# Norms with the tokens on partitions, and another start for the first unit, in a two-block forward kernel

## The reference

```
x = x + 0.5 * swiglu(rms(x, ffn1_norm), w1, w3, w2)          # ffn1, hidden width 2816
x = x + (gate_a * rwkv7(h) + gate_b * fox(h)) @ w_out        # h = rms(x, mix_norm)
x = x + 0.5 * swiglu(rms(x, ffn2_norm), ...)                 # ffn2
x = rms(x, final_norm)
mod = silu(c) @ w_ada + b_ada                                # shifts, scales and gates of block two
x   = x   + 0.5 * g1 * swiglu(rms(x, .)   * (1 + sc) + sh, ...)   # ffn3, main tokens
ctx = ctx + 0.5 * g1 * swiglu(rms(ctx, .) * (1 + sc) + sh, ...)   # ffn3, 256 context tokens, same weights
x = x + g2 * merge(retention(x, ctx), fourier(x))            # ret_q, ret_k, ret_v, four_in, ... out2
x = x + 0.5 * g3 * swiglu(rms(x, .) * (1 + sc) + sh, ...)    # ffn4
return rms(x, norm_final)
```

## Time and profile before

| | |
|---|---|
| median of 3 runs | 1769.89 µs (1769.77 to 1769.99) |
| the profiled execution | 1771.81 µs, its span 1770.0 µs |
| PE busy | 1704.9 µs, 96% of the span |
| DVE, ACT busy | 1059.6 µs (60%), 652.3 µs (37%) |
| granted TensorE clock, mean over the span | 0.991 of full |
| read from HBM | 265.48 MB, 151 GB/s over the span |

### The profile page before, as it was taken

One profiled execution on the slowest core, in us unless ns is written; L12 is line 12 of the kernel. 1 busy time (PEld: TensorE's weight loads), 2 busy tenths in 40 slices (PEclk: granted clock), 3 DMA queues, 4 the chain that ended last, 5 costly groups with the idle time before them and its releaser, 6 DMA issues.

```text
span 1770.0 us, 32228 instructions
## 1 busy us (share of the span) xinstructions
PE 1704.9 (96%) x13366; PEld 1552.1 (88%) x13366; DVE 1059.6 (60%) x1570; ACT 652.3 (37%) x763; POOL 5.2 (0%) x13
## 2 busy tenths in 40 slices
PE   6999999899999999999999999899999999999997
PEld 6999898676998999998888888888889799989997
DVE  6766747542766766765465465942356634676766
ACT  4333446222544333432222212522346334443332
POOL 0000000000000000000000000000000000000000
PEclk9999999999999999999999999999999999999999
DMA  6545566476244545422222222232223235445551
GB/s 245 190 175 185 193 257 240 152 283 256 100 165 171 190 168 187 166 85 105 95 95 95 95 95 96 95 119 104 90 96 106 97 143 185 176 151 184 185 190 48
DMA packets 37537, 267.74 MB, mean 151 GB/s; under 512 B 4192, under 2 KB 4448, under 8 KB 5456
## 3 DMA queue, kind: packets, MB, share of 16 engines
q1 hardware_dynamic: 36432, 262.37, 40.8%
q0 software_dynamic: 1024, 4.17, 0.6%
HBM read 265.48 MB, written 1.05 MB: 151 GB/s over the span
## 4 chain that ended last, share of the span: by engine, by line
PE 92%; DVE 4%; ACT 2%; issue 1%; DMA 1%; DVEq 0%; POOL 0%; SPq 0%; ACTq 0%
PE PS L329 25%; PE PS L330 24%; PE PS L331 24%; PE PS L542 2%; PE PS L543 2%; PE PS L544 2%; PE PS L562 2%; PE PS L981 2%; PE PS L407 1%; PE PS L1014 1%; PE PS L1001 1%; ACT W_HI L316 1%; PE PS L783 1%; DVE RSTD L1467 1%; PE PS L968 1%
## 5 line engine op out<-in xcount | busy, mean ns | idle before, releaser
L329 PE MATMUL PS<-H_HI,W_HI 128*128 128x256 f32 (+1 forms) x2128 | 652.0, 306 | 21.0 <-DVE H_LO L1459 11.9
L330 PE MATMUL PS<-H_LO,W_HI 128*128 128x256 f32 (+1 forms) x2128 | 647.0, 304 | 0.0
L331 PE MATMUL PS<-H_HI,W_LO 128*128 128x256 f32 (+1 forms) x2128 | 646.8, 304 | 0.0
L316 ACT ACTIVATE W_HI<-RAW 128x2048 fp32r<-128x2048 f32 x213 | 407.2, 1912 | 585.0 <-PE PS L331 553.9
L324 DVE TENSOR_TENSOR W_LO<-RAW,W_HI 128x2048 fp32r<-128x2048 f32 x213 | 487.3, 2288 | 189.4 <-ACT W_HI L316 188.9
L329 PEld LDWEIGHTS PS<-H_HI,W_HI 128*128 128x128 f32 x2128 | 411.2, 193 | 43.8 <-issue 27.6
L330 PEld LDWEIGHTS PS<-H_LO,W_HI 128*128 128x128 f32 x2128 | 411.5, 193 | 15.4 <-issue 0.2
L331 PEld LDWEIGHTS PS<-H_HI,W_LO 128*128 128x128 f32 x2128 | 411.1, 193 | 14.9
L329 PE MATMUL PS<-HID_HI,W_HI 128*128 128x256 f32 (+1 forms) x704 | 218.4, 310 | 3.3 <-DVE XC L1509 3.3
L330 PE MATMUL PS<-HID_LO,W_HI 128*128 128x256 f32 (+1 forms) x704 | 217.9, 309 | 0.0
L331 PE MATMUL PS<-HID_HI,W_LO 128*128 128x256 f32 (+1 forms) x704 | 217.8, 309 | 0.0
(11 more groups left out here) (315 smaller groups left out, 1713.8 us busy)
## 6 DMA issues: line engine op xcount, KB each, us to landing
RAW<-stream SPq DMA_DIRECT2D x249, 1024.0 KB, 4.8
XC<-xin SPq DMA_DIRECT2D x2, 512.0 KB, 5.0
XC<-xin POOLq DMA_DIRECT2D x1, 1024.0 KB, 5.1
out<-NT POOLq DMA_DIRECT2D x2, 512.0 KB, 2.9
CON<-consts POOLq DMA_DIRECT2D x1, 548.0 KB, 6.0
LW<-lora POOLq DMA_DIRECT2D x1, 512.0 KB, 6.6
DFT<-dft POOLq DMA_DIRECT2D x1, 512.0 KB, 3.8
ROPE<-rope POOLq DMA_DIRECT2D x1, 256.0 KB, 3.4
```

What stands on the lines that cost most here:

```text
L316: nc.scalar.activation(W_HI[s % RING][:], RAW[u % RING][:], ACT.Copy).then_inc(hi_done, 1)
L329: nc.tensor.matmul(acc, w_hi, x_hi, start=first, stop=False)
L330: nc.tensor.matmul(acc, w_hi, x_lo, start=False, stop=False)
L331: return nc.tensor.matmul(acc, w_lo, x_hi, start=False, stop=last)
```

## The change

The norms get their sums with the tokens on the partitions. PE takes the squares as the fixed operand and a vector of ones as the moving one (`ONE3`, two columns wide), a half of the tokens at a time, and leaves 128 by 2. Root and reciprocal run on 128 by 2. Then PE spreads the result over the partitions again with two matmuls against the identity (`norm_spread`), and DVE scales from PSUM. All eight tiles are scaled, then all eight low halves made; the first unit behind a norm starts with the products of `H_HI` and multiplies `H_LO` behind them. nd and ne become one chain: eight sums with four columns (the squares and the squares times the square of nd's gain) within `up_ctx(0)`, and the norm ne is gone as a pass of its own. In front of ffn2 and ffn4 two of the three sums go into the last output tile, and `keep_clock` issues matmuls whose result nobody reads around the third.

The rest: four transfers for the first tokens and two for unit 0, whose `W_LO` GpSimd makes and PE multiplies last; seven matmuls on a constant at the start (`WARM`); the split of the second unit behind a norm moves behind the last addition into `XC`; the last `down` of ffn3 does the main tokens and then the context (`down_last`), the norm ng between them; `ret_q` has other banks, nh other places; one `w_ada` unit moves from in front of `fox_qk` into the inversion (`ada(16)`); SP stores the output in four transfers.

```diff
-ADA_INV = 23
-ADA_AFTER = {PHASE["fox_qk"] - 1: 3, PHASE["fox_v"] + 1: ADA_INV}
+ADA_INV = 24
+ADA_AFTER = {PHASE["fox_qk"] - 1: 2, PHASE["fox_v"] + 1: ADA_INV}
...
+            for q in range(4):
+                sp.dma_start(XC[:, 0, 2 * q:2 * q + 2], xin[0, :, 2 * q:2 * q + 2]).then_inc(S(f"x_in{q}"), 16)
...
+            for h in range(2):
+                sp.dma_start(by_k(RAW[0])[:, :, 4 * h:4 * h + 4], by_k(stream[0])[:, :, 4 * h:4 * h + 4])\
+                    .then_inc(landed[0] if h else S("half_in"), 16)
...
+            for k in range(0, KT, 2):
+                sp.wait_ge(S("final"), k + 2)
+                sp.dma_start(out[:, k:k + 2], NT[:, k:k + 2]).then_inc(S("stored"), 16)
...
+            pool.wait_ge(S("half_hi"), 1)
+            pool.wait_ge(hi_done, 1)
+            nc.gpsimd.tensor_tensor(W_LO[0][:], RAW[0][:], W_HI[0][:].bitcast(F32), ALU.subtract).then_inc(lo_done, 1)
             pool.dma_start(CON[:, 256:], consts[:, 256:]).then_inc(S("masks_in"), 16)
...
                 pe.wait_ge(S("norm_sq"), KT * NORM[name] + k + 1)
-                last = nc.tensor.matmul(NORM_BANK[name], con("ones"), tmp[:, k], start=(k == 0), stop=(k == 7))
+                w = 4 if name == "nd" else 2
+                for tt in range(2):
+                    last = nc.tensor.matmul(sums(name), tmp[:, k, tt * P:(tt + 1) * P], SQW[:, k, 2 - 2 * tt:6 - 2 * tt] if w == 4 else
+                                            ONE3[:, 1 - tt:3 - tt], start=(k == first and tt == 0), stop=(k == last_k and tt == 1))
...
+            def keep_clock(n, bank):
+                for _ in range(n):
+                    nc.tensor.matmul(BK8[bank][:, 0:ROWS], con("ident"), CON[:, 0:ROWS], start=True, stop=True)
+            def norm_spread(name):
+                pe.wait_ge(S("norm_rec"), NORM[name] + 1)
+                for q in ((2, 3, 0, 1) if name == "nd" else (0, 1)):
+                    last = nc.tensor.matmul(spread_of(name)[:, q * P:(q + 1) * P], RSTD[:, q:q + 1].to_broadcast([P, P]), con("ident"),
+                                            start=True, stop=True)
+                last.then_inc(S("norm_spread"), 1)
...
+                            if t == 0 and k % 2:
+                                norm_sum("nd", 4 * w + k // 2)
...
+                    if t == 0:
+                        for k in range(KT):
+                            pe.wait_ge(S("norm_hi"), KT * NORM_H[h_name] + k + 1)
+                            for w in range(2):
+                                c = (w * KT + k) * P
+                                two(tile(w), W_HI[sl][:, c:c + P], W_LO[sl][:, c:c + P], H_HI[:, 0, k], k == 0)
+                    if t == 0:
+                        for k in range(KT):
+                            pe.wait_ge(S("norm_h"), KT * NORM_H[h_name] + k + 1)
...
+                    for q, t in ([(q, 0) for q in range(4)] + [(q, 1) for q in range(4)] +
+                                 [(q, t) for q in range(4, 16) for t in range(2)]):
+                        h, m = q // 8, q % 8
...
+                        if q == 9:
+                            norm(then)
+                        if q == 11:
+                            norm_spread(then)
...
                 if halves == 2:
                     up_ctx(0)
-                    norm(h_name)
-                    up_ctx(1)
+                    up_ctx(1, (0,))
+                    norm_spread("nd")
+                    up_ctx(1, (1,))
...
+            pe.wait_ge(S("warm_in"), 1)
+            for _ in range(7):
+                nc.tensor.matmul(BK8[0][:, 0:ROWS], WARM[:, 0:P], WARM[:, P:P + ROWS], start=True, stop=True)
+            pe.wait_ge(S("one3"), 1)
+            for k in (6, 7, 0):
+                norm_sum("na", k, first=6, last_k=0)
             pe.wait_ge(S("con_in"), 16)
-            norm("na")
+            keep_clock(1, 0)
+            norm_spread("na")
+            keep_clock(2, 0)
             ffn(0, "ffn1", 1, "na", "nb")
-            ada(12)
+            ada(4)
+            norm_spread("nb")
+            ada(4)
...
             for n in range(NC):
                 z_step(n)
-            ada(12)
+            ada(16)
...
-                 behind={3: lambda: norm("nc")})
+                 within={(7, 4): lambda: norm_sum("nc", 0), (7, 6): lambda: norm_sum("nc", 6)})
+            keep_clock(2, 0)
+            norm_sum("nc", 7)
+            keep_clock(1, 0)
+            norm_spread("nc")
+            keep_clock(2, 0)
...
-            split_hi(act, 0)
+            act.wait_ge(S("half_in"), 16)
+            A(by_k(W_HI[0])[:, :, 0:4], by_k(RAW[0])[:, :, 0:4], ACT.Copy).then_inc(S("half_hi"), 1)
+            act.wait_ge(landed[0], 16)
+            A(by_k(W_HI[0])[:, :, 4:8], by_k(RAW[0])[:, :, 4:8], ACT.Copy).then_inc(hi_done, 1)
...
             def norm_rows(name, half, gain, shift=None, tmp=NT):
-                for k in range(KT + 2):
-                    if k < KT:
-                        scale(name, half, k, gain, tmp)
-                    if k >= 2:
-                        rest(name, half, k - 2, shift, tmp)
+                dve.wait_ge(S("norm_spread"), NORM[name] + 1)
+                for k in range(KT):
+                    scale(name, half, k, gain, tmp)
+                for k in range(KT):
+                    rest(name, half, k, shift, tmp)
...
-                split_lo(dve, s0 + 34)
-                add(10, range(8), m0 + 124)
+                if halves == 1:
+                    add(10, range(8), m0 + 124)
...
-            split_lo(dve, 0)
             norm_rows("na", 0, lambda k: par("n1", k))
+            dve.wait_ge(lo_done, 1)
             split_lo(dve, 1)
...
-            norm("nb", 0, lambda k: par("nm", k))
+            split_lo(dve, PHASE["fox_qk"] + 1, part=0)
+            reciprocal("nb")
+            split_lo(dve, PHASE["fox_qk"] + 1, part=1)
+            norm_rows("nb", 0, lambda k: par("nm", k))
```

277 lines of the change are left out of this document (206 added, 71 removed).

## The result

The changed kernel took 1759.08 us (median of 4 runs, 1758.39 to 1759.72) against 1769.83 before: ratio 0.9941, 95% interval 0.9926 to 0.9957. It is faster, by 10.8 us where 18.7 were forecast, and lies 1.1 us outside the range.

A forecast was written before the change was run, and what follows sets the result against it. PE was taken as the bound, busy 1704.9 of 1770.0 µs and waiting nearly always for norms. Gains of 24.3 less costs of 5.6 gave 18.7, so 1753.1 profiled and a median of 1751.2; range 1747 to 1758.

The forecast's parts named there:

- The fourth `w_ada` unit: In the inversion: its load must wait for a free buffer, so PE waits 3.2 µs, plus 1.0 for the clock.
- nd, ne and ng: Norms: nd and ne as one chain, gain 2.8 µs; ng under the context's tiles, with what follows, gain 4.5.
- End: Last norm and output store: shorter reciprocal and root, an added spread, smaller last transfer; gain 2.2 µs.
- One of the signs that I had set for being wrong: At the start, unit 1 of ffn1 waiting for GpSimd beyond 20 µs would show the forecast wrong.
- Start: First norm and unit 0 of ffn1: GpSimd's subtraction taken as 2.29 µs, unit 1 at 19.9 instead of 26.3, gain 6.4.
- The rival that the two hold each other up: At the start, DVE's low halves wait for GpSimd's subtraction: nothing lost, 1752.1 to 1753, or 1761 µs; chance 0.17.
- The rival's price, 20.8: When unit 1 of ffn1 begins if GpSimd takes twice DVE's time and holds up its low halves: 20.8 µs.
- Costs: Losses at nf (a spread, 0.4 µs) and in the inversion (an added `w_ada` unit, its wait and clock): 5.6 in all.
- The rival "the clock is not held": Small sums count as PE idle: gain gone at nc and ni, half speed at nb, nd or ng; 1757 to 1759, chance 0.14.
- nc and ni: Norms before ffn2 and ffn4: two sums inside the last tile, high pass first, no 1.2 GHz; gains 2.7 and 1.7 µs.
- nb: Norm behind ffn1: 1.66 wait gone, last addition +0.7, first product +4.15; gain 4.0 µs, 0.93 of it only moved.
- The base: Whole kernel: profiled execution before took 1771.8 µs, and the median was taken to lie 1.9 under it.

The follow-up runs named there:

- e12: Changed kernel with the moved `w_ada` unit behind the first unit of `fox_qk` instead of in the inversion: 1757.26 µs, ratio 0.9935 to the kernel before.
- e1: Changed kernel with unit 0's low half made by DVE behind its token low halves, GpSimd computing nothing: 1759.35 µs, ratio 0.9942 to the kernel before.
- e3: Changed kernel with four dense `keep_clock` products in PE's wait in front of the sums of nf: 1756.85 µs, ratio 0.9927 to the kernel before.
- e8: Changed kernel with GpSimd making only half of unit 0's low half, DVE the rest behind its token low halves: 1759.64 µs, ratio 0.9943 to before.
- e6: Changed kernel with three dense fp32 products in PE's wait in front of the sums of nb: 1759.24 µs, ratio 0.9943 to the kernel before.
- e2: Changed kernel with the `w_ada` units where they stood before, three behind ffn1 and three in the inversion: 1759.78 µs, ratio 0.9943 to before.
- e4: Changed kernel with the first two sums of nc and ni behind the last tile, not inside it: 1755.89 µs, ratio 0.9918 to before.
- e7: Changed kernel with the sums of nc and ni behind the last tile and no `keep_clock` at either: 1759.32 µs, ratio 0.9943 to before.
- e9: Changed kernel with the edits of e3, e4, e6, e8 and e12 together: 1746.73 µs, ratio 0.9879 to the kernel before.

## Why the prediction was right or wrong

Right: the direction, and about half of the places. **The fourth `w_ada` unit** waited 3.30 us (forecast 3.2), with 1.1 lost to the clock behind it (1.0); e12 shows both to be the price of that place. **nd, ne and ng** came to 3.29 and 4.48 against 2.8 and 4.5. The reciprocal is 0.17, the 1.66 gaps are gone, the clock is 1.00 behind ng and ni (at ni it fell in e1 and e3, with the same code there), and the tile of `out` waits 0.92 inside (1.0). **End**: 2.87 against 2.2. The norm gave 1.1 of the 1.25 expected; from the end of the last scaling to the end of the span it is 2.64 us instead of 4.40, 1.8 less, where I had allowed 0.95 for the transfers.

Wrong, by step. The sum misses 6.6 us, 3.2 of them at the start, 1.6 at nc, 1.4 at nf, 1.3 at nb and 0.6 at ni, less what nd, ne, the end and the inversion gave beyond the forecast. One of the signs that I had set for being wrong, unit 1 waiting for GpSimd beyond 20, came true.

- **Start, "Its floor is DVE's for the same tile, 2.29 ... I take 2.29, the same form".** It is 4.57, and I had set the longer time aside because by it "the sum stays". The Trainium skill, GPSIMD Engine Reference, "3. Performance versus the Vector engine", gives 4497 ns, and the trace agrees with its 4.57 us. The sum stays only if GpSimd's time lies beside DVE's. The rival that the two hold each other up was the true case, and my forecast had the overlap wrong: the first low half took 2.93 instead of 0.41, and e1 shows why. The Trainium skill, SBUF — State Buffer, "Who interferes with whom", says that a VectorE instruction with two SBUF inputs contends with a GpSimd one that reads SBUF, and that one with at most one SBUF input, outside the modes that use two ports, doesn't; by that rule both come out right, the low halves held up and the scalings of e8 (one operand in PSUM) at 3.22. The low half was held to the end of GpSimd's instruction, and 0.29 beyond.
  The rival's price, 20.8, was too small by 2.3. GpSimd started 1.4 later than the 11.2 of the forecast: "Unit 0 has landed whole at about 10.0" was read from the kernel before, where the unit is one transfer, and the change has two, behind two more for the tokens; the second half landed at 11.38. With that the low halves ended at 19.82 instead of 18.5 and the split of unit 1 at 22.02 instead of 20.8. The last 1.1 is the clock, for which the forecast's own sum had charged 1.6. That the scaling started at 11.40, not 10.0, cost nothing more, as the first low half ended with GpSimd's row in any case.
- **Costs, "nf gets a spread, 0.4".** The spread costs that (e3). But I had looked for a lost clock only where PE waits over 4 us. At nf the same wait of 1.69 had left the clock at 1.00 in front of wide sums and doesn't in front of sums of 2 columns. The rival "the clock is not held" named the mechanism, and put it at nc and ni, nb, nd and ng, not at nf. What it costs at nf is 1.6 in this profile and 3.1 in six others. That rival's time, 1757 to 1759, lies close to the 1759.08 measured, by luck: of its terms only a part of nc's is in this profile, and nearly half of the sum's miss lies at the start, which it left as it was.
- **nc and ni, "PE waits there 1.0 µs inside the tile and the third sum comes 1.7 later" and "no 1.2 GHz".** The third sum came 2.6 later, since the clock wasn't held and `keep_clock` stood in front of it at 1.2 GHz; where the clock held (e6) it came 2.0 later. nc gained 1.1 for 2.7, 1.0 of the miss for the clock. At ni the clock held, the third sum came 2.0 later there too, and the gain was 1.1 for 1.7; the rest of that wasn't looked at. That the sums should never have been in the tile (worth 1.5 at each) I hadn't asked.
- **nb, "last addition +0.7".** It was +1.7: I took the additions to follow PE, where DVE alternates them with the squares at 0.67 a block, in the kernel before too. The first product came at +5.6 instead of +4.15, and the gain was 2.7 for 4.0. I had also not seen that the moved split frees its buffer of the stream 6 us later, counted from the start of `down` (load issued 10.6 us behind it instead of 4.5); the change doesn't pay for it at nb, since it has one `w_ada` unit less there, but in the inversion, where that unit went.
- **The base.** 1.3 us: the profiled execution of before stood 1.98 over its median, the other 0.64. That is the spread between executions and no fault of the mechanism.

## What to carry to other kernels

- When narrow instructions replace wide ones on TensorE behind a wait, look at the granted clock there, however short the wait: at nf it fell in ten of ten profiles behind 1.69 us of waiting and 12 matmuls of 2 columns, and in none of three with dense products in that wait. Look at every place that has the new form, not only at the long gaps.
- A unit that is moved out of one stall needs a place with dense work in front of it and a free buffer. And an instruction that frees a buffer can't be moved later for nothing: ask which load waits for it. With the split moved behind the additions, the load that had been issued at 209.48 was issued at 213.22 (e2).
- GpSimd was help for VectorE under instructions that take an operand from PSUM (e8); beside two-input ones from SBUF its work held them up (e1). And an instruction put inside a tile to save time behind it delays that tile, on which the whole tail hangs.
- A landing read from the kernel before holds only while the transfers ahead of it stay as they are.

## What the runs showed that was not expected

The clock falls at different places in executions of the same code. nb held it in the change, in e4 and in e7 and lost it in seven others that have nothing added in the wait there either; nf lost 3.4 us at half speed in some and 6.8 in others. The kernel before took 1766.2 to 1772.2 in 11 executions timed together, with mean clocks of 0.990 to 0.994. The clock isn't all of that spread: the slowest of them, 1772.15, had 0.993, and the fastest, 1766.19, 0.994; what the rest is stays open. A local gain of up to 5.6 us (e12) can be lost from sight in it. Filled and dense, e9's four executions lay within 1.8 us (1745.16 to 1746.96) at clocks of 0.995 to 0.997.

What stays open: which part the `w_ada` units (32 columns of weights) have in the fall at nb was not tried apart, nor whether the gain of e9 over the sum of its parts' medians is all clock. Three `w_ada` units at nb with the split put back in front of the additions were not tried under the new norm.
